# A two-layer streaming encoder step: first norm from token rows, parameter loads on two queues, another VectorE order in the FFN

## The chip, the cores and the metric

The kernel runs on 1 core of a Trainium2 chip. The metric is device time in microseconds (us) of one execution, smaller is better; TensorE is called PE here, VectorE DVE, ScalarE ACT, GpSimd POOL, SyncE SP.

## The reference

1,024 prompt frames and 32 frames of running streams, of width 1,024, go through two layers. Layer 0 mixes by a convolution module, layer 1 by attention in a sliding window; each mixer is followed by a gated FFN of inner width 2,816. Everything is in float32.

```python
def rms_norm(x, g):
    return x * lax.rsqrt(jnp.mean(x * x, axis=-1, keepdims=True) + RMS_EPS) * g
# layer 0
h = rms_norm(x, g_mix[0])
a, gate = jnp.split(h @ w_pw1 + b_pw1, 2, axis=-1)
g = concat([state or zeros, a * sigmoid(gate)])       # 30 frames of state
c = depthwise_conv31(g, w_dw) + b_dw
x = x + silu(layer_norm(c, ln_g, ln_b)) @ w_pw2 + b_pw2
x = x + (silu(h @ w_gate[0]) * (h @ w_up[0])) @ w_down[0]      # h = rms_norm(x, g_ffn[0])
# layer 1: 16 query heads, 4 key heads of 64, RMS norm of q and k per head
s = q @ k.T * SCALE - slope * distance, masked to own and two previous chunks of 64
p = exp(s - m) / (sum(exp(s - m)) + exp(sink - m))
x = x + (p @ v) @ w_o
x = x + FFN of layer 1
```

Also returned are the last 30 gated frames of both inputs and the last 128 keys and values.

## The kernel before, in words

The activations lie with channels on partitions: `x` holds 8 tiles (k = 0 to 7) of 128 channels by tokens. Tokens come in two halves, A (512) and B (512 and the 32 of the running streams, 544). A float32 product is made of three: every weight tile 128x1024 is loaded by SP into `raw` (two buffers), ACT's `hi()` (L795) copies it to `whi`, and POOL's `lo()` (L1797) takes the rest, `wlo`; activations likewise are split in `hAh`, `hAl`, `hBh`, `hBl`. A projection (`proj`) adds, for 8 tiles k, high·whi and low·whi (L327), and then 8 times high·wlo (L336). The FFN's way down does so with act·h and act·l (L522, L529).

PSUM's 8 banks are two rings of 4. A tile of half A takes one bank, one of half B two, so of B only two fit into a ring; a bank is taken when its user before it has freed it, in the order of the program.

**The start.** SP loads token rows `x_in` 0 to 8 into `stage`, ACT 17 small parameters into `R`. PE transposes x in groups of four 128x128 (`x_group`, L369), ACT (`x_in_place`, L878) and DVE (L1316) copy them to `x` and square them (`sqx`); PE sums the squares over channels with a matrix of ones (`square_mean`, L359), ACT makes Ln and Exp of the mean (`factor`), and `norm_parts` has DVE multiply (L1297), ACT copy the high half (`n_hi_part`), DVE subtract the low half (L1302). The second norm, `mix0B`, has its squares on ACT and their sums on POOL (`sum_squares`, L1807).

**SEQ1** is a list of 29 projections of `w_pw1`, gate and value in turn; half A's come first. Each pair is gated (`sigmoid`, L901, and `glu`), then the 31 taps of the convolution run beside: a tap is either a DVE operation in PSUM (L1389) or an ACT product (L920) added by POOL (L1828); `NP` says how many taps are products, `conv_a_steps` how many operations go beside each projection. At its end POOL's `csum` feeds the mean of the LayerNorm (L345 on PE). Then come `w_pw2` (p2) of half A, the FFN of half A with half B's convolution beside it, and so on: each half's FFN has the other half's mixer beside it.

**An FFN group** (`FFN 0A`, `0B`, `1A`, `1B`; G = 0 to 10) makes two pairs of gate and up projections and then, for the group before, eight tiles of the way down (D, d = 0 to 7), each added to x by DVE (`add_to_x`, L1468). Attention for the other half stands between, in steps of four units b: `read_scores` on DVE (L1496 to L1509), exps with their sums on ACT (`exps`, L1031), the division on DVE (`scale_probs`, L1533 and L1537), transposes, values, `out_low` on DVE. `act_low` (L1480) makes the low half of the gated activation. No planner sets the order; each engine's program lists it, and semaphores join the lists.

## Time and profile before

| what | us |
|---|---|
| time, median of 3 runs (range) | 2412.67 (2409.51 to 2414.92) |
| profiled execution, its own time | 2410.06 |
| profiled execution, span | 2408.2 |
| PE busy | 2284.0 (95%) |
| DVE busy | 1208.4 (50%) |
| POOL busy | 1120.4 (47%) |
| ACT busy | 979.0 (41%) |

The page has the span in slices, the chain of work that ended last, and groups of instructions with their releasers; "L327" is the source line. A duration stands in us, a mean in ns. A wait is put down to the event that came last. Matmuls are pipelined, so that the mean durations of their records overlap.

### The profile page before, as it was taken

The numbers are of one execution on the slowest core, as the hardware profiler recorded it, in microseconds if no ns is written. First come the engines' busy times: TensorE is split into PE (matmuls) and PEld (weight loads), VectorE is DVE, ScalarE is ACT, GpSimd is POOL, SyncE is SP. The second block draws the span as 40 slices with busy tenths as digits, with TensorE's granted clock in tenths as the row PEclk, the third lists the DMA queues.
The fourth block names the chain that finished last, engine by engine and source line by source line (L and its number), as shares of the span: only waits on it lengthen the run. The fifth ranks groups of instructions, "written<-read, shape, count | busy, mean of one in ns | idle before, by whom it ended". The sixth has DMA issues, their size and how long they took to land.

```text
span 2408.2 us, 34667 instructions
## 1 busy us (share of the span) xinstructions
PE 2284.0 (95%) x14027; PEld 2038.8 (85%) x14027; DVE 1208.4 (50%) x1924; ACT 979.0 (41%) x1511; POOL 1120.4 (47%) x588
## 2 busy tenths in 40 slices
PE   6897888999899999999999999999999999999999
PEld 5797666888789799899989889888888889999998
DVE  4687657883435335655563344556565342232233
ACT  4554644443423643433343356444444333222222
POOL 2799458996345533323233553333333343333332
PEclk8999899999999999999999999999999999999999
DMA  3111122233232322222222232222222322332222
GB/s 124 53 45 53 53 62 83 88 97 97 81 94 88 89 82 70 62 71 69 63 65 83 82 88 77 87 71 79 79 71 79 87 80 91 95 97 88 88 80 90
DMA packets 311436, 191.53 MB, mean 80 GB/s; under 512 B 40214, under 2 KB 285550, under 8 KB 311278
## 3 DMA queue, kind: packets, MB, share of 16 engines
q1 hardware_dynamic: 309168, 188.18, 26.3%
q8 instruction: 112, 1.84, 0.3%
q10 hardware_dynamic: 2110, 1.14, 0.2%
q14 instruction: 46, 0.38, 0.1%
HBM read 184.39 MB, written 5.10 MB: 79 GB/s over the span
## 4 chain that ended last, share of the span: by engine, by line
PE 81%; DVE 6%; POOL 6%; ACT 3%; issue 3%; DMA 0%; ACTq 0%; POOLq 0%; DVEq 0%
PE ps L327 37%; PE ps L336 19%; PE ps L522 12%; PE ps L529 6%; POOL accp L1828 4%; PE ps L492 2%; DVE x L1468 1%; PE ps L478 1%; PE ps L452 1%; PE ps L345 1%; PE ps L359 1%; DVE sco L1537 1%; DVE sq L1297 1%; POOL wlo L1797 1%; POOL rs L1807 1%
## 5 line engine op out<-in xcount | busy, mean ns | idle before, releaser
L1797 POOL TENSOR_TENSOR wlo<-raw,whi 128x1024 fp32r<-128x1024 f32 x342 | 825.4, 2414 | 1203.3 <-PE ps L336 838.9
L795 ACT ACTIVATE whi<-raw 128x1024 fp32r<-128x1024 f32 x342 | 361.4, 1057 | 715.0 <-PE ps L327 410.3
L327 PE MATMUL ps<-hBh,whi 128*128 128x272 f32 x2112 | 441.4, 290 | 16.2 <-ACT s L901 9.4
L327 PE MATMUL ps<-hAh,whi 128*128 128x512 f32 x1056 | 422.3, 400 | 34.9 <-DVE hAl L1302 15.5
L327 PE MATMUL ps<-hBl,whi 128*128 128x272 f32 x2112 | 439.9, 290 | 0.0
L327 PE MATMUL ps<-hAl,whi 128*128 128x512 f32 x1056 | 419.3, 397 | 0.0
L327 PEld LDWEIGHTS ps<-hBh,whi 128*128 128x128 f32 x2112 | 334.5, 190 | 19.8 <-ACT s L901 9.8
L1468 DVE TENSOR_TENSOR x<-ps,x 128x512 f32<-128x512 f32 (+1 forms) x368 | 252.2, 701 | 189.1 <-PE ps L529 131.3
L327 PEld LDWEIGHTS ps<-hBl,whi 128*128 128x128 f32 x2112 | 332.9, 189 | 0.0
L336 PE MATMUL ps<-hBh,wlo 128*128 128x272 f32 x2112 | 294.5, 292 | 0.0
L336 PEld LDWEIGHTS ps<-hBh,wlo 128*128 128x128 f32 x2112 | 273.5, 188 | 6.2 <-issue 1.9
L327 PEld LDWEIGHTS ps<-hAh,whi 128*128 128x128 f32 x1056 | 202.1, 191 | 89.4 <-issue 23.0
L336 PE MATMUL ps<-hAh,wlo 128*128 128x512 f32 x1056 | 273.5, 401 | 0.5 <-POOL wlo L1797 0.5
L1475 DVE TENSOR_TENSOR s<-ps,s 128x512 f32<-128x512 f32 (+1 forms) x88 | 62.3, 708 | 417.2 <-PE ps L336 415.2
L336 PEld LDWEIGHTS ps<-hAh,wlo 128*128 128x128 f32 x1056 | 196.4, 189 | 49.2 <-issue 4.3
L327 PEld LDWEIGHTS ps<-hAl,whi 128*128 128x128 f32 x1056 | 202.8, 192 | 40.9
L1828 POOL TENSOR_TENSOR accp<-accp,prod 128x512 f32<-128x512 f32 (+1 forms) x152 | 210.0, 1381 | 26.0 <-ACT prod L920 11.8
L1019 ACT ACTIVATE pth<-ps 128x512 fp32r<-128x512 f32 (+1 forms) x64 | 36.6, 571 | 194.1 <-PE ps L478 194.1
L1389 DVE SCALAR_TENSOR_TENSOR ps<-gxB,dwc,ps 128x574 f32<-128x574 f32 x152 | 113.9, 808 | 0.0
L1547 DVE TENSOR_TENSOR ptl<-ps,pth 128x512 fp32r<-128x512 f32 (+1 forms) x64 | 42.1, 658 | 122.5 <-ACT pth L1019 122.5
L1537 DVE TENSOR_SCALAR sco<-sco,small 128x256 f32<-128x256 f32 (+2 forms) x132 | 101.3, 809 | 2.3
L522 PE MATMUL ps<-act0h,whi 128*128 128x272 f32 (+1 forms) x288 | 79.0, 329 | 18.3 <-DVE x L1468 16.5
(233 smaller groups left out, 3277.4 us busy)
## 6 DMA issues: line engine op xcount, KB each, us to landing
raw<-in_w_gate_dram SPq DMA_DIRECT2D x88, 512.0 KB, 3.8
raw<-in_w_up_dram SPq DMA_DIRECT2D x88, 512.0 KB, 3.8
raw<-in_w_down_dram SPq DMA_DIRECT2D x88, 512.0 KB, 3.6
raw<-in_w_pw_dram SPq DMA_DIRECT2D x38, 512.0 KB, 4.0
raw<-in_w_qkv_dram SPq DMA_DIRECT2D x32, 256.0 KB, 3.7
raw<-in_w_o_dram SPq DMA_DIRECT2D x64, 128.0 KB, 2.9
stage<-in_x_prompt_dram SPq DMA_DIRECT2D x8, 512.0 KB, 7.7
raw<-in_w_qkv_dram SPq DMA_DIRECT2D x8, 512.0 KB, 3.7
```

Source lines behind the costliest of these rows:

```text
L327: ins = nc.tensor.matmul(o, whi[n % 2][:, P * k:P * (k + 1)], src[:, k, c0:c0 + w], start=(k == 0 and src is hi_[h]), stop=False)
L336: ins = nc.tensor.matmul(o, wlo[n % 2][:, P * k:P * (k + 1)], hi_[h][:, k, c0:c0 + w], start=False, stop=(k == KD - 1))
L492: ins = nc.tensor.matmul(ps[0:HD, 6, 0:256], v[:, slot, HD * g:HD * (g + 1)], p[:, 256 * z:256 * (z + 1)], start=(z == 0 and w == 0), stop ...
L522: ins = nc.tensor.matmul(o, whi[n % 2][:, wc], src[s + e][:, c0:c0 + w], start=(e == 0 and src is ach), stop=False)
L529: ins = nc.tensor.matmul(o, wlo[n % 2][:, wc], ach[s + e][:, c0:c0 + w], start=False, stop=(e == 1))
L795: nc.scalar.activation(whi[n % 2][:], raw[n % 2][:], ACT.Copy).then_inc(w_hi, 1)
L1389: link(nc.vector.scalar_tensor_tensor((X, Y)[q % 2], two(gx[h][:, c, t:t + w]), dwc[:, KD * t + c:KD * t + c + 1], (X, Y)[q % 2], ALU.mult ...
L1468: nc.vector.tensor_tensor(xd, pt(key), xd, ALU.add).then_inc(fr(key), 1)
L1475: nc.vector.tensor_tensor(s, pt(key), s, ALU.mult).then_inc(fr(key), 1)
L1537: ins = nc.vector.tensor_scalar(pr, pr, den[:, 2 * b + s:2 * b + s + 1], None, ALU.mult)
L1797: nc.gpsimd.tensor_tensor(wlo[n % 2][:], raw[n % 2][:], f(whi[n % 2][:]), ALU.subtract).then_inc(w_lo, 1)
L1828: nc.gpsimd.tensor_tensor(accp[p % 2][:, 0:w], accp[p % 2][:, 0:w], prod[r % 2][:, 0:w], ALU.add).then_inc(padd, 1)
```

## The change

In the first norm, ACT takes the square and its sum of each token row (`row_squares`, one value per token), Ln and Exp of it (`row_factor`), DVE makes of each 128 values a diagonal, and 32 float32 matmuls of a chunk of `stage` with a diagonal give the transposed and scaled x in PSUM (`xn`). ACT scales by the gain into the high half, DVE subtracts into the low half. For half B the diagonals are multiplied by ones on PE (`row_factors`) and copied to `rs`. The 17 parameter loads become 7 on ACT's queue and 8, with the sinks, on SP's; the later five x loads wait for `x_in[3]`; the distance, bias and mask work moves into later slots. Half A has one product less per channel and one chain operation more (10 for 11).

```python
-            want = 0 if s in (0, 1, 6) else 1 if s == 7 else 6 if s < 6 else 7
+            want = 0 if s < 2 else 1 if s in (5, 6) else 6 if s < 5 else 7
-NP = {"A": 11, "B": 10}
+NP = {"A": 10, "B": 10}
+            for k in range(KD):
+                b = take(("xn", k), "A", 1 - k % 2)
+                for t in range(4):
+                    pe.wait_ge(diag_ready, t + 1)
+                    ins = nc.tensor.matmul(ps[:, b, P * t:P * (t + 1)], stage[t][:, P * k:P * (k + 1)],
+                                           diag[:, t, :], start=True, stop=True)
+                ins.then_inc(pfull[b], 1)
...
+                nc.scalar.activation(junk[t % 2][0:w, :], stage[t][0:w, :], ACT.Square, accum_out=ssq[0:w, t:t + 1]
+                                     ).then_inc(row_sq, 1)
...
-                if s in (6, 7):
-                    if s == 6:
-                        factor("mix0B")
-                    for k in range(4 * (s - 6), 4 * (s - 5)):
+                if s in (5, 6):
+                    for k in range(4 * (s - 5), 4 * (s - 4)):
                         n_hi_part("mix0B", k)
...
             factor("ffn0A")
+            sigmoid(sig)
             for k in range(KD):
                 n_hi_part("ffn0A", k, ("p2", "A", KD - 1))
                 if k == 3:
-                    sigmoid(sig)
                     hi()
...
+                                if G == 1:
+                                    state_rows(b)
...
                         taps("B", CONV_B[G, 4][1])
-                        norm_b(G, 4)
...
+                        scale_probs(att, cur, 0)
                         exps(att, cur, 2)
+                        scale_probs(att, cur, 1)
                         exps(att, cur, 3)
                     if G:
                         hi()
+                    if (l, h) == (0, "A") and G:
+                        norm_b(G, 4)
...
+                    for d in range(KD):
+                        if G:
+                            add_to_x(("D", l, h, G - 1, d))
+                        if d == 1:
+                            read_scores(att, cur, 3)
+                        if d == 2:
+                            out_low(att, prev, 3)
+                        if d == 3:
+                            act_low(l, h, G, 1)
+                        if G and d % 2:
+                            denominators(att, cur, d // 2)
```

`scale_probs` is on ACT now, a Copy with a scale, after DVE's `denominators`, which is the reciprocal alone. The mean of `ffn0A` takes its bank before gate B2's projection, the mean of `lnB` ring 1; the state rows, four in a row after group 0, are spread over group 1's projections. POOL has seven `sum_squares` fewer.

PE at the start, before, from the parameters' transposes to the first two tiles of the first projection (L327 is `proj`, `sqx` the squares, `ones_d` the matrix of ones):

```order
L379 MATMUL ps<-ident,R 128x82 [waits pfree0,params_in]
L381 MATMUL ps<-ident,R 128x120 x2
L386 MATMUL ps<-ident,R 128x124 [waits pfree1]
L386 MATMUL ps<-ident,R 128x124
L359 MATMUL ps<-sqx,ones_d 128x512 [waits sq_ready,pfree2]
L359 MATMUL ps<-sqx,ones_d 128x512 [waits sq_dve]
L359 MATMUL ps<-sqx,ones_d 128x512 [waits sq_ready]
L359 MATMUL ps<-sqx,ones_d 128x512 [waits sq_dve]
L359 MATMUL ps<-sqx,ones_d 128x512 [waits sq_ready]
L359 MATMUL ps<-sqx,ones_d 128x512 [waits sq_dve]
```


And after, with one group of transposes behind the parameters and the diagonals (`diag`) as what streams through PE; L337 is `proj`:

```order
L403 MATMUL ps<-ident,R 128x40 [waits params_in]
L405 MATMUL ps<-ident,R 128x120 x2
L410 MATMUL ps<-ident,R 128x124 x2
L392 MATMUL ps<-ident,stage 128x128 [waits x_in3,pfree2]
L392 MATMUL ps<-ident,stage 128x128 x3
L392 MATMUL ps<-ident,stage 128x128 [waits pfree3]
L392 MATMUL ps<-ident,stage 128x128 x3
L418 MATMUL ps<-diag,stage 128x128 [waits diag_ready] x4
L418 MATMUL ps<-diag,stage 128x128 [waits diag_ready,pfree0]
L418 MATMUL ps<-diag,stage 128x128 [waits diag_ready] x7
```


The means of squares stood between the transposes and the projection; the diagonal matmuls stand there now, and none of them waits for `sqx`.

DVE at the end of an FFN group of half B with attention of half A (group 2 of FFN 0B), before: `out_low` (L1562) stands some rows higher, here stand the last score update, `act_low` (L1480), and then two sums into x (L1468), a reciprocal and two scalings for each pair:

```order
L1500 ISA small 128x1
L1509 TENSOR_SCALAR bias<-bias 128x256 [waits dv]
L1509 TENSOR_SCALAR bias<-bias 128x256
L1480 TENSOR_TENSOR act1l<-s,act1h 128x544 [waits act_hi]
L1468 TENSOR_TENSOR x<-ps,x 128x544 [waits pfull0]
L1468 TENSOR_TENSOR x<-ps,x 128x544 [waits pfull2]
L1533 RECIPROCAL small<-small 128x2 [waits e_ready]
L1537 TENSOR_SCALAR sco<-sco,small 128x128 [waits dv]
L1537 TENSOR_SCALAR sco<-sco,small 128x128
L1468 TENSOR_TENSOR x<-ps,x 128x544 [waits pfull0]
L1468 TENSOR_TENSOR x<-ps,x 128x544 [waits pfull2]
```


And after, behind two sums into x (not shown), where L1573 is `add_to_x`, L1637 the reciprocal, L1585 `act_low`, L1661 `out_low`, L1605 and L1614 `read_scores`:

```order
L1601 COPY sco<-nsink 128x2 [waits t_full]
L1605 ISA sco,small<-ps,bias,nsink 128x256 [waits s_full]
L1605 ISA small 128x1
L1605 ISA sco,small<-ps,bias,nsink 128x256
L1605 ISA small 128x1
L1614 TENSOR_SCALAR bias<-bias 128x256 [waits dv]
L1614 TENSOR_SCALAR bias<-bias 128x256
L1637 RECIPROCAL small<-small 128x2 [waits e_ready]
L1573 TENSOR_TENSOR x<-ps,x 128x544 [waits pfull2]
L1661 TENSOR_TENSOR hAl<-ps,hAh 64x2x128 [waits o_hi]
L1573 TENSOR_TENSOR x<-ps,x 128x544 [waits pfull0]
L1585 TENSOR_TENSOR act1l<-s,act1h 128x544 [waits act_hi]
```


Two sums stand ahead of the scores' read now, two more ahead of `act_low`, which stood ahead of all eight.

ACT at the end of the same kind of group, before: exps of four units (L1031, two each) and the two weight copies (L795):

```order
L1031 ACTIVATE sco,small<-sco,small 128x257 [waits s_read]
L1031 ACTIVATE sco,small<-sco,small 128x257
L795 ACTIVATE whi<-raw 128x1024 [waits whi_free,w_in0]
L1031 ACTIVATE sco,small<-sco,small 128x257 [waits s_read]
L1031 ACTIVATE sco,small<-sco,small 128x257
L1031 ACTIVATE sco,small<-sco,small 128x257 [waits s_read]
L1031 ACTIVATE sco,small<-sco,small 128x257
L795 ACTIVATE whi<-raw 128x1024 [waits whi_free,w_in1]
```


And after, where L840 is the weight copy, L1083 the exps and L1095 the scaling:

```order
L840 ACTIVATE whi<-raw 128x1024 [waits whi_free,w_in0]
L1095 ACTIVATE sco<-sco,small 128x128 [waits den_ready]
L1095 ACTIVATE sco<-sco,small 128x128
L1083 ACTIVATE sco,small<-sco,small 128x257 [waits s_read]
L1083 ACTIVATE sco,small<-sco,small 128x257
L1095 ACTIVATE sco<-sco,small 128x256 [waits den_ready]
L1095 ACTIVATE sco<-sco,small 128x256
L1083 ACTIVATE sco,small<-sco,small 128x257 [waits s_read]
L1083 ACTIVATE sco,small<-sco,small 128x257
L840 ACTIVATE whi<-raw 128x1024 [waits whi_free,w_in1]
L1095 ACTIVATE sco<-sco,small 128x256 [waits den_ready]
```


Scaling of units 0 and 1 stands between the exps of 1, 2 and 3 and thus ahead of the second weight copy; units 2 and 3 stand behind it.

## Rows read from the trace of the kernel before

**Rows 1.** Page, part 4: shares of the chain that ended last, by line.

```profile
PE ps L327 37%; PE ps L336 19%; PE ps L522 12%; PE ps L529 6%; POOL accp L1828 4%; PE ps L492 2%; DVE x L1468 1%; PE ps L478 1%; PE ps L452 1%; PE ps L345 1%; PE ps L359 1%; DVE sco L1537 1%; DVE sq L1297 1%; POOL wlo L1797 1%; POOL rs L1807 1%
```

**Rows 2.** Waits of PE, 0 to 350 us: total, times, longest (us).

```profile
PE ps L327 <- DVE hAl L1302: 15.5, 11, 7.1
PE ps L345 <- POOL csum L1850: 12.4, 1, 12.4
PE ps L327 <- ACT s L901: 9.4, 2, 9.2
PE ps L345 <- ACT s L901: 5.7, 1, 5.7
...
PE ps L379 <- DMA R<-in_state_conv_dram: 2.7, 1, 2.7
```

**Rows 3.** Timeline of the start: start, us, engine, what [idle before].

```profile
4.59 3.65 PE L369 MATMUL ps<-ident,stage 128*128 128x128 f32 x16 [4.59 <-DMA stage<-in_x_prompt_dram]
...
19.54 8.64 PE L359 MATMUL ps<-sqx,ones_d 128*128 128x512 f32 x16
...
28.27 1.28 ACT L819 ACT_TABLE_LOAD   x1 [8.02 <-PE ps L359]
...
33.34 0.77 PE L327 MATMUL ps<-hAh,whi 128*128 128x512 f32 x1 [5.16 <-DVE hAl L1302]
```

**Rows 4.** Timeline of PE alone: transposes of x, the mean after the convolution.

```profile
43.26 4.01 PE L369 MATMUL ps<-ident,stage 128*128 128x128 f32 x20
...
52.57 2.08 PE L369 MATMUL ps<-ident,stage 128*128 128x128 f32 x20
...
239.96 2.07 PE L345 MATMUL ps<-csum,ones_d 128*128 128x512 f32 x2 [12.40 <-POOL csum L1850]
```

**Rows 5.** Windows: each engine busy (instructions), PEclk, DMA share, GB/s.

```profile
19.50:22.80 3.30, 3.30 (x6) 1.40 (x5) 3.29 (x7) 0.75 (x1) 3.30 (x2) 0.51 0.10 40
22.90:28.20 5.30, 5.29 (x13) 2.06 (x11) 1.96 (x4) 0.00 (x0) 1.44 (x2) 1.00 0.68 198
33.30:47.30 14.00, 12.11 (x37) 8.78 (x38) 8.60 (x13) 6.00 (x10) 0.00 (x0) 0.52 0.00 1
367.00:403.00 36.00, 27.24 (x116) 20.72 (x115) 20.51 (x30) 15.76 (x23) 26.86 (x17) 0.95 0.27 80
```

**Rows 6.** Groups by line and shape: count, busy, mean ns, idle before.

```profile
L795 ACT ACTIVATE whi<-raw 128x1024 fp32r<-128x1024 f32 x342 | 361.4, 1057 | 715.0 <-PE ps L327 410.3 <-PE ps L522 301.4 <-DMA raw<-in_w_gate_dram 3.0
...
L1828 POOL TENSOR_TENSOR accp<-accp,prod 128x512 f32<-128x512 f32 x80 | 103.3, 1292 | 20.4 <-ACT prod L920 11.5 <-POOL accp L1828 0.4
L1389 DVE SCALAR_TENSOR_TENSOR ps<-gxA,dwc,ps 128x512 f32<-128x512 f32 x144 | 96.4, 747 | 0.0
...
L1031 ACT ACTIVATE sco<-sco,small 128x257 f32<-128x257 f32 x112 | 55.4, 498 | 0.1
```

**Rows 7.** Waits of PE, 350 to 800 us.

```profile
PE ps L327 <- ACT cvo L1232: 7.3, 4, 2.0
PE ps L327 <- ACT whi L795: 5.4, 1, 5.4
```

**Rows 8.** Chain of waits in order of time: start, us, piece.

```profile
654.89 6.77 PE ps L327 x16
...
734.99 4.03 PE ps L327 x32
```

**Rows 9.** Waits of PE, 800 to 1330 us.

```profile
PE ps L522 <- DVE x L1468: 23.2, 17, 2.2
```

**Rows 10.** Waits of PE, 1990 us to the end.

```profile
PE ps L522 <- DVE x L1468: 9.0, 10, 0.9
```

**Rows 11.** Timeline: two act_low of VectorE, one lo of GpSimd.

```profile
1063.25 0.71 DVE L1480 TENSOR_TENSOR act1l<-s,act1h 128x544 fp32r<-128x544 f32 x1
...
2112.79 1.58 DVE L1480 TENSOR_TENSOR act3l<-s,act3h 128x544 fp32r<-128x544 f32 x1 [0.72 <-ACT act3h L990]
...
2119.13 2.41 POOL L1797 TENSOR_TENSOR wlo<-raw,whi 128x1024 fp32r<-128x1024 f32 x1 [5.35 <-ACT whi L795]
```

More of the change, by code:

```diff
@@ L138, in build @@
             sqx = sb("sqx", [P, KD, 512], F32, c)
+        with ExitStack() as c:
+            junk = [sb(f"junk{s}", [P, D], F32, c) for s in range(2)]
+            diag = sb("diag", [P, 9, P], F32, c)
         with ExitStack() as c:
@@ L236, in pt @@
         def pt(key, rows=P):
-            b, _, h = place[key]
+            b, _, h, _ = place[key]
             if h == "A":
@@ L814, in factor @@
                 full(act, key)
-                if ev in ON_PE and i:
+                if ev in ON_PE:
                     old = EV[i - 1]
@@ L829, in n_hi_part @@
                     full(act, after)
-                act.wait_ge(xn_ready, KD * sum(e[:2] != "ln" for e in EV[:i]) + k + 1)
+                act.wait_ge(xn_ready, KD * sum(e[:2] != "ln" and e != "mix0A" for e in EV[:i]) + k + 1)
                 nc.scalar.activation(hi_[h][:, k, :], nrm[k % 2][:, dest(h)], ACT.Copy).then_inc(h_hi[h], 1)
@@ L1033, in exps, with scale_probs @@
                                          accum_out=den[:, 2 * b + s:2 * b + s + 1]).then_inc(e_ready, 1)
+            def scale_probs(h, beta, b):
+                if not 0 <= beta or b >= n_units(h, beta):
+                    return
+                u, _, _, _, _, nk, _ = unit(h, beta, b)
+                nk = nk if beta < 8 else WIN + TS
+                act.wait_ge(den_ready, u + 1)
+                for s in range(2):
+                    pr = sco[b][:, s, 1:1 + nk]
+                    ins = nc.scalar.activation(pr, pr, ACT.Copy, scale=den[:, 2 * b + s:2 * b + s + 1])
+                ins.then_inc(p_ready, 1)
             def q_high(h, i):
@@ new lines, in late_params @@
+            def late_params():
+                full(dve, ("par", 2))
+                b = place["par", 2][0]
+                nc.vector.tensor_copy(col[:, 40:NCOL], ps[:, b, 0:42]).then_inc(fr(("par", 2)), 1)
+                freed(dve, ("par", 2))
+                nc.vector.tensor_scalar(gqn, col[:, C_QN:C_QN + 1], -SCALE, None, ALU.mult).then_inc(col_ready, 1)
+                dve.wait_ge(sinks_in, 16)
+                for i in range(4):
+                    r = slice(TS * i, TS * (i + 1))
+                    ins = nc.vector.tensor_scalar(ssink[r, :], nsink[r, i:NH:4], -1.0, None, ALU.mult)
+                ins.then_inc(sink_ready, 1)
+                dve.wait_ge(sink_ready, 1)
+                nc.vector.tensor_scalar(nsink[:], nsink[:], -1.0, None, ALU.mult).then_inc(sink_ready, 1)
@@ L1681, in ffn @@
                         q_low(att, 7)
-                    out_low(att, prev, 3)
-                    read_scores(att, cur, 3)
-                    act_low(l, h, G, 1)
                     if (l, h, G) == (1, "A", NG - 1):
```

360 lines of the change are left out of this document (207 added, 153 removed).

## The prediction

> **What bounds the kernel now.** I read the chain that ended last first: over half of it is TensorE (PE) in the projections of L327 and L336, then the FFN's second product (L522, L529), and what is not PE is small and named: GpSimd's accp (POOL L1828) 4%, VectorE's sums into x (L1468) 1% [rows 1]. So the time is that of PE's work plus the gaps in it, and I price the change gap by gap. The waits of PE in the first 350 us show five large gaps, 45.7 us together: 15.5 behind the low halves of the first norm, 12.4 once behind GpSimd's csum at the end of the first convolution, 9.4 (9.2 of it in one wait, before the FFN's first projection) and 5.7 behind ScalarE's sigmoid, 2.7 behind the parameters' DMA [rows 2]. The rows of the start tell what the first gap is made of: transposes from 4.59 on, the means of the squares from 19.54, ScalarE's table at 28.27, the first projection at 33.34, and its first 16 matmuls spread out until 43.26, where the next transposes stand [rows 3, 4]. The clock there was 0.51 to 0.52 of full speed, that is the 1.2 GHz level, in the first 3.3 us of L359 and again from 33.3 to 47.3 [rows 5].
>
> **Part 1, the first norm (start to the convolution's mean).** Removed: transposes as the only source of the squares, L359's 8.64 us, and the chain VectorE, ScalarE, VectorE that paces the first projection, four pairs of channel tiles in 9.9 us (33.34 to 43.26). Added: a Square with sum for each of four token rows as they land. No row shows that; a copy of the same 128x1024 on ScalarE takes 1.06 [rows 6], twice that is my upper end; I take 1.24, near the copy. With x landing from 4.59 and a table load of 1.28 [rows 3], the squares end near 10.8 (10 to 15). Ln and Exp act on 4 columns, with the table 2.0: 12.8. Four diagonals and the parameter transposes lie beside or cost about 1: the diagonal matmuls start near 14. They leave 64 records (32 matmuls, two records each). The nearest rows are the 20 transposes of the same tile: 0.104 each at 52.57, 0.20 each at 43.26 [rows 4], so 6.7 if all run at the upper level and 12.8 if none does. L359 began at 0.51 for 3.3 us and ran on at 1.00 [rows 5]; treated so, 16 records take 3.3 and 48 take 5.0, 8.3. New weights in each could cost more, so I take 10.5 (6.7 to 20): 24.5. The 16 matmuls of the first projection then stand behind one another, 3.8 with the last low half: they end near 28.4, not 43.26: **-15**.
>
> The Trainium skill (TensorE: Matmul & The Clock Gate, Part 4: PE-mode transpose) says that transposes don't count as PE work for the clock gate. The trace agrees so far as L359 ran at 0.51 right behind 32 transposes; by that rule the diagonal matmuls begin low, and without it the step would take 6.7, 3.8 less than in my sum.
>
> From there to the mean at 239.96 [rows 4]: the 5.7 wait (GpSimd's sums of squares for the second norm, which go) is gone, and the x transposes at 43.26 take 2.08, not 4.01 [rows 2, 4]. But ScalarE and VectorE have more squares and diagonals at the same steps, so I give 1.5 back: **-6**. Then the 12.4 wait. GpSimd loses 8 products of 1.29 [rows 6] and seven sums, of about the same length by shape: 10.3 + 9.3 = 19.6. With a start 15 earlier it could end 35 earlier; PE, with 21 off, is what would stop it, and VectorE gains 8 operations of 0.67 (96.4/144) [rows 6], 5.4 us, and in the last step 17 in place of 11. So the wait shrinks, it doesn't go: 12.4 to 7.5: **-5**. In all **-26** (-10, if GpSimd or the second norm holds PE as before, to -35).
>
> **Part 2, parameters on two queues.** The 2.7 wait lies in the 15 already: it is off the path once diagonals are later than landing. What moves, iota, biases and masks, goes to ScalarE and GpSimd in the second stage's norm slots, where both wait for PE; without that cover it is 8 ScalarE operations and 13 small ones of GpSimd, some 5 us. On SP's queue the small loads stand ahead of x4 to x8, which now also wait for x3; PE first needs x4 one projection later than before. **0** (0 to +3).
>
> **Part 3, the FFN's first norm and the state rows.** The sigmoid now stands before the norm's parts and the bank is taken earlier, so the 9.2 wait ends when the mean and its Ln and Exp do, 2.7 behind: **-6.5** (-3 to -8). The state rows are spread over the next group's projections: in 367 to 403 PE was busy 27.24 of 36 [rows 5], 7.3 of the rest in four waits for ScalarE's cvo [rows 7]. Spread, each copy has a projection for cover: **-9** (-6 to -11). In group 8, ScalarE's weight copies stood behind the norm's parts: 5.4 [rows 7], and the 16 matmuls behind took 6.77 where 32 of 272 columns take 4.03 [rows 8], by columns 3.8 for these, so 3.0 more at the low clock. With the copies first: **-8** (-5 to -8.4).
>
> **Part 4, FFN order and scaling.** In FFN 0B PE waits 23.2 in 17 waits for L1468 [rows 9]; VectorE was late because read_scores, act_low and scaling stood between sums into x. Now two sums come first, then read_scores, sums, out_low, act_low. Scaling leaves VectorE; on ScalarE a 128x257 pass takes 0.498 [rows 6], so 132 passes of a little less cost some 60 us of ScalarE's idle time: 0 while the second weight copy isn't held up. What is late next is act_low: at 1063.25 it took 0.71, at 2112.79 1.58, with GpSimd's L1797 beside it (2.41 long, as at 2119.13) [rows 11]. By the new order two sums 1.5 apart, the read of the scores, a reciprocal, two more sums and out_low come ahead of it: it starts 7.1 behind the first sum in 0B by my estimate, GpSimd's low weights at 6.9: held to 9.3, ended at 9.9, which costs PE 1.6 and with the read before it 1.85 a group; ten groups, 18.5 against 23.2: **-5** (-20 if VectorE starts first, 0 if more is held). In FFN 1B there are ten waits, 9.0 in all [rows 10]; the pieces before act_low are fewer there, it starts 0.06 before GpSimd: **-9** (+7 if behind, 1.6 for each group).
>
> **Sum**: -26 - 6.5 - 9 - 8 - 5 - 9 = -63.5 from the profiled execution's own 2410.06 (span 2408.2): 2346.6. The median of before, 2412.67, is 2.6 above that execution; I add half of this: **2348**.
>
> **Rivals.** (a) *GpSimd first in both FFNs.* Every act_low in the third place stands behind L1797: FFN 0B gives 0, FFN 1B costs 7, and with a start worth 18 only: 2410 - 18 - 6.5 - 9 - 8 + 7 = 2375. For it: the 1.58 row; against: 0.71 is as often seen, and in 1B the order by 0.06 us is mine, from a schedule that shifts. The Trainium skill (SBUF — State Buffer, Who interferes with whom) says that a VectorE operation with two SBUF inputs shares a read port with GpSimd, that one of them waits for the other's end, and that sums with one input in PSUM don't. The two act_low rows agree. Rows 11 alone give the 1.6.
> (b) *VectorE first in both, and the start at its better end*: -30 - 7 - 9 - 8 - 20 - 9 = -83, 2327. For it: VectorE's share is 50% and it loses all of L1537. Against: the first part's copies.
> (c) *Slower: ScalarE's queue.* It runs in order; scaling unit 1 waits for VectorE's reciprocal, behind act_low, and ahead of it stand the last exps and the second weight copy. If that copy comes over a projection late (4.03 for 32 of its 48 matmuls, so 6 us), PE waits as at group 8, 5.4 + 3.0 = 8.4 [rows 7, 8], in each of 20 groups with attention: +168, and with the gains of parts 1 and 3, 2410 - 49.5 + 168 = 2529; it decides from the point where the reciprocal is 6 us late. Against: act_low held by GpSimd is 2.4 late, and the second copy waits for PE to free its buffer anyway.
> (d) *The start's gain doesn't arrive*: the second norm and GpSimd hold PE in the first stage until the mean stands where it stood, part 3 gives its least, 3 + 6 + 5, and act_low costs its 7: 2410 - 14 + 7 = 2403, at the edge of no change. For it: GpSimd is the releaser of the 12.4; against: it loses 19.6 of work before that.
>
> **How the numbers follow.** Forecast 0.53, its own range 2335 to 2365; (a) 0.22; (b) 0.16; (c) 0.06; (d) 0.03. The range 2320 to 2385 takes in (a), (b), the forecast and the ends of the diagonal matmuls' cost, and leaves out (c), (d) and the tails. About 0.2% (5 us) is what a measurement here tells from no change: faster 0.53 + 0.22 + 0.16 = 0.91, same 0.03, slower 0.06.
>
> **What would show it.** Right: the first L327 near 25 and the mean of the convolution near 214, not 239.96; waits for cvo and for the weight copy at group 8 gone; L1468's waits in 0B about 18, in 1B near 0, with VectorE's act_low there 0.71 long. A clock at half level under the diagonal matmuls makes part 1 6 to 8 us worse. Act_low at 1.6 to 2.4 in 1B is (a). Wrong: PE waiting for whi in the attention groups (c), or the csum wait still over 12 (d).

## The result, and the profile after

The changed kernel takes 2324.2 us, median of four runs (2323.93 to 2325.04), against 2411.59 (2409.51 to 2414.92) for the kernel before on the same chip: a ratio of 0.9637, 95% interval 0.9620 to 0.9654, 87 us less. 2348 was forecast, with a range of 2320 to 2385. The time lies in the range, outside the forecast's own range (2335 to 2365), and 3 us from rival (b), 2327.

The profiled execution spans 2322.2 us, 86.0 less than before. By the page's totals PE is busy 2263.4 us instead of 2284.0, so 65.4 of the 86.0 us is idle time (124.2 us before, 58.8 after). How much of the other 20.6 is less work and how much the clock the totals don't tell; the mean granted clock was 0.983 before and 0.989 after. The page's chain, shares by line:

```profile
PE ps L337 41%; PE ps L346 21%; PE ps L553 14%; PE ps L560 7%; PE ps L523 2%; POOL accp L1920 2%; PE ps L483 1%; PE ps L509 1%; PE ps L355 1%; PE ps L484 1%; PE ps L485 1%; POOL wlo L1889 1%; PE ps L372 1%; DVE x L1573 1%; DVE sq L1382 1%
```

Against [rows 1] the projections' shares (L337 and L346 are L327 and L336 of before) grew by 4 and 2 points, and the scaling on VectorE has left the chain.

Where the 86 us came from, by the start of an instruction that both traces have:

```
                                             before    after    shift   in the stage   forecast
mean after the first convolution             239.96   214.12   -25.8      -25.8         -26
first way down (D) of FFN 0A                 402.58   358.41   -44.2      -18.3         -6.5 - 9
last way down of FFN 0A                      712.57   661.69   -50.9       -6.7         -8
first way down of FFN 0B                     916.11   866.53   -49.6       +1.3          0
first way down of FFN 1A                    1538.17  1466.73   -71.4      -21.9         -5
first way down of FFN 1B                    2034.54  1961.71   -72.8       -1.4          0
end of the span                             2408.2   2322.2    -86.0      -13.2         -9
```

Two stages carry the miss: FFN 0B, 17 us more than forecast, and FFN 1B, 4 more. The +1.3 is a stretch of PE at a granted clock of 0.60, so mostly at the 1.2 GHz level (768.4 to 772.0), behind a wait of 1.9; the runs below with the squares early, with the same program there, don't have it, and why it comes is not shown.

The start. These are rows of the timeline of PE (start, duration, what, idle time before it), for what [rows 3, 4] show of before:

```profile
16.42 9.27 PE L418 MATMUL ps<-diag,stage 128*128 128x128 f32 x64 [1.61 <-DVE diag L1415]
25.45 0.48 PE L337 MATMUL ps<-hAh,whi 128*128 128x512 f32 x1
...
35.04 2.35 PE L392 MATMUL ps<-ident,stage 128*128 128x128 f32 x20
...
214.12 2.08 PE L355 MATMUL ps<-csum,ones_d 128*128 128x512 f32 x2 [9.01 <-POOL csum L1942]
```

The diagonal matmuls start at 16.4, 2.4 later than forecast, take 9.27 where 10.5 was taken, and the first projection starts at 25.45 (24.5 forecast). What they waited for stands in VectorE's rows:

```profile
13.19 0.20 DVE L1407 COPY col<-ps 128x40 f32<-128x40 f32 x1 [2.56 <-PE ps L405]
...
15.46 1.50 DVE L1415 TENSOR_SCALAR diag<-ident,small 128x128 f32<-128x128 f32 x4
```

The factor was there at 12.34. PE's transposes of the parameters waited for their DMA until 12.54; VectorE stood idle 2.56 us for them, then copied the parameters (13.19) and the two groups of x that PE transposes behind them, and only then made the diagonals.

The 16 matmuls of the first projection stand one behind the other until 29.3; before it was 43.26. The windows of PE (length, then busy time of PE, PEld, DVE, ACT, POOL, then the clock) show that the first 2.6 us of L418 ran at the 1.2 GHz level, as L359 had begun [rows 5]:

```profile
16.40:19.00 2.60, 2.58 (x12) 2.58 (x13) 0.56 (x3) 0.46 (x1) 0.00 (x0) 0.50 1.01 413
19.00:25.70 6.70, 6.70 (x55) 6.70 (x55) 4.46 (x7) 5.08 (x8) 2.37 (x1) 0.90 0.48 147
```

The waits of PE, first from 0 to 300 us, then from 300 to 750 and from 750 to 1300 (total, times, longest):

```profile
PE ps L355 <- POOL csum L1942: 9.0, 1, 9.0
PE ps L337 <- DVE hAl L1387: 8.3, 7, 7.1
PE ps L337 <- ACT s L951: 4.8, 1, 4.8
...
PE ps L403 <- DMA R<-in_state_conv_dram: 2.6, 1, 2.6
...
PE ps L346 <- POOL wlo L1889: 2.9, 1, 2.9
PE ps L337 <- DVE hAl L1387: 2.6, 2, 1.3
...
PE ps L553 <- DVE x L1573: 3.9, 3, 1.3
```

Of [rows 2] the low halves of the first norm are gone (8.3 is the next norm's, 7.1 of it one wait; of the 15.5 of before 8.2 were that norm's already), the wait for csum fell from 12.4 to 9.0, and the one before the FFN from 9.2 to 2.6 in two. The 5.7 for a sigmoid is not gone: PE waits 4.8 for one at 65.12, its only wait above a microsecond between the first projection and the one for csum. Two others that the kernel before had in this stretch are gone:

```profile
PE ps L327 <- ACT whi L795: 2.9, 1, 2.9
PE ps L327 <- DVE gxA L1350: 0.9, 1, 0.9
```

Of [rows 7] both are gone, but a wait for GpSimd's low weights, 2.9, is new. The sums into x held PE 17 times for 23.2 us in FFN 0B [rows 9] and now 3 times for 3.9; in FFN 1B ten times for 9.0 [rows 10], and now not once (1900 us to the end).

**A wait costs more than its length.** In FFN 1B the waits were 0.9 each, but each group became 1.2 shorter. Rows of PE's timeline, of before and then of after, from the first matmul of a way down to the projection behind it:

```profile
2111.07 0.42 PE L522 MATMUL ps<-act0h,whi 128*128 128x272 f32 x2
...
2115.15 0.49 PE L522 MATMUL ps<-act0h,whi 128*128 128x272 f32 x2 [0.89 <-DVE x L1468]
...
2124.29 0.42 PE L327 MATMUL ps<-hBh,whi 128*128 128x272 f32 x2
```

```profile
2035.74 0.41 PE L553 MATMUL ps<-act0h,whi 128*128 128x272 f32 x2
...
2047.75 0.41 PE L337 MATMUL ps<-hBh,whi 128*128 128x272 f32 x2
```

2124.29 - 2111.07 = 13.22 and 2047.75 - 2035.74 = 12.01: 1.21 for a wait of 0.89, so 0.3 more, which the profile shows as no idle time. In ten groups that is 3.2 of the 4 us that FFN 1B gave beyond its forecast.

**In FFN 0B a race decides.** Two groups of FFN 0B, timeline of VectorE, GpSimd and PE:

```profile
1002.04 0.72 DVE L1573 TENSOR_TENSOR x<-ps,x 128x544 f32<-128x544 f32 x1 [1.40 <-PE ps L560]
...
1006.27 0.42 DVE L1661 TENSOR_TENSOR hAl<-ps,hAh 64x256 fp32r<-64x256 f32 x1
...
1007.23 2.40 POOL L1889 TENSOR_TENSOR wlo<-raw,whi 128x1024 fp32r<-128x1024 f32 x1 [4.87 <-ACT whi L840]
1007.36 2.85 DVE L1585 TENSOR_TENSOR act1l<-s,act1h 128x544 fp32r<-128x544 f32 x1
...
1011.06 0.49 PE L553 MATMUL ps<-act2h,whi 128*128 128x272 f32 x2 [1.31 <-DVE x L1573]
...
1094.36 0.72 DVE L1573 TENSOR_TENSOR x<-ps,x 128x544 f32<-128x544 f32 x1 [1.40 <-PE ps L560]
...
1098.48 0.40 DVE L1661 TENSOR_TENSOR hAl<-ps,hAh 64x256 fp32r<-64x256 f32 x1
...
1099.50 0.71 DVE L1585 TENSOR_TENSOR act1l<-s,act1h 128x544 fp32r<-128x544 f32 x1
1099.55 2.94 POOL L1889 TENSOR_TENSOR wlo<-raw,whi 128x1024 fp32r<-128x1024 f32 x1 [4.87 <-ACT whi L840]
```

The rows at 1002.04 and 1094.36 are the first sums of the two groups. In the first group GpSimd starts 0.13 ahead, VectorE's act_low lasts 2.85, and PE waits 1.31. In the second group VectorE starts 0.05 ahead, act_low lasts 0.71, GpSimd is the one that is longer (2.94 for 2.40), and PE doesn't wait. Of the eight groups with attention and a way down, three are like the first (a way down of 13.8 us) and five like the second (12.2 to 12.3; before, 15.3 and once 16.0). The prediction had GpSimd first in all.

Which groups lose is no chance: GpSimd starts 5.19 behind the first sum in both, and VectorE comes 0.18 later in the first because of `out_low` (L1661). It starts 0.73 behind the start of the sum ahead of it (1005.54), not 0.62 (1097.86), and the next sum 0.45 behind it, not 0.38. The three groups are those whose `out_low` finishes an odd key head and so writes to partitions 64 to 127 (`r = slice(HD * (g % 2), ...)` in the kernel); four of the five have an even one, and the first has none. The same groups have the longer steps in the runs below. Why the one for an odd head starts later is open.

### The profile page after: what moved, and what is told of

Same layout as the page of the kernel before. It is cut to its first block, busy times and chain, and to the rows that moved or that the text cites. A ratio compares the mean times of both kernels' runs of the same rounds, so it can differ in the third digit from the quotient of the medians.

```text
span 2322.2 us, 34761 instructions
## 1 busy us (share of the span) xinstructions
PE 2263.4 (97%) x14082; PEld 2034.6 (88%) x14082; DVE 1096.5 (47%) x1802; ACT 1024.8 (44%) x1639; POOL 1114.9 (48%) x573
## 3 DMA queue, kind: packets, MB, share of 16 engines
q8 instruction: 113, 1.85, 0.3%
## 4 chain that ended last, share of the span: by engine, by line
PE 91%; POOL 3%; DVE 2%; ACT 2%; issue 1%; DMA 0%; ACTq 0%; DVEq 0%; POOLq 0%
PE ps L337 41%; PE ps L346 21%; PE ps L553 14%; PE ps L560 7%; PE ps L523 2%; POOL accp L1920 2%; PE ps L483 1%; PE ps L509 1%; PE ps L355 1%; PE ps L484 1%; PE ps L485 1%; POOL wlo L1889 1%; PE ps L372 1%; DVE x L1573 1%; DVE sq L1382 1%
## 5 line engine op out<-in xcount | busy, mean ns | idle before, releaser
L1889 POOL TENSOR_TENSOR wlo<-raw,whi 128x1024 fp32r<-128x1024 f32 x342 | 839.7, 2455 | 1131.6 <-PE ps L346 802.9
L840 ACT ACTIVATE whi<-raw 128x1024 fp32r<-128x1024 f32 x342 | 361.6, 1057 | 638.7 <-PE ps L337 379.7
L337 PE MATMUL ps<-hBh,whi 128*128 128x272 f32 x2112 | 440.2, 289 | 8.2 <-DVE x L1573 3.3
L337 PE MATMUL ps<-hBl,whi 128*128 128x272 f32 x2112 | 439.4, 289 | 0.0
L337 PE MATMUL ps<-hAh,whi 128*128 128x512 f32 x1056 | 417.9, 396 | 18.5 <-DVE hAl L1387 10.9
L337 PE MATMUL ps<-hAl,whi 128*128 128x512 f32 x1056 | 415.4, 393 | 0.0
L1573 DVE TENSOR_TENSOR x<-ps,x 128x512 f32<-128x512 f32 (+1 forms) x368 | 258.3, 705 | 243.9 <-PE ps L560 181.4
L337 PEld LDWEIGHTS ps<-hBh,whi 128*128 128x128 f32 x2112 | 332.9, 189 | 11.4 <-issue 5.0
L337 PEld LDWEIGHTS ps<-hBl,whi 128*128 128x128 f32 x2112 | 331.6, 189 | 0.0
L346 PE MATMUL ps<-hBh,wlo 128*128 128x272 f32 x2112 | 293.7, 291 | 0.0
L346 PEld LDWEIGHTS ps<-hBh,wlo 128*128 128x128 f32 x2112 | 273.0, 188 | 6.3 <-issue 1.9
L346 PE MATMUL ps<-hAh,wlo 128*128 128x512 f32 x1056 | 275.0, 403 | 2.9 <-POOL wlo L1889 2.9
L337 PEld LDWEIGHTS ps<-hAh,whi 128*128 128x128 f32 x1056 | 200.3, 190 | 67.9 <-DVE hAl L1387 11.1
L346 PEld LDWEIGHTS ps<-hAh,wlo 128*128 128x128 f32 x1056 | 196.7, 190 | 51.7 <-issue 4.3
L337 PEld LDWEIGHTS ps<-hAl,whi 128*128 128x128 f32 x1056 | 200.8, 190 | 39.9
L1920 POOL TENSOR_TENSOR accp<-accp,prod 128x512 f32<-128x512 f32 (+1 forms) x144 | 200.2, 1390 | 25.3 <-ACT prod L970 12.5
L1489 DVE SCALAR_TENSOR_TENSOR ps<-gxA,dwc,ps 128x512 f32<-128x512 f32 x152 | 101.8, 748 | 0.0
```

The lines of the kernel that those rows point to most:

```text
L337: ins = nc.tensor.matmul(o, whi[n % 2][:, P * k:P * (k + 1)], src[:, k, c0:c0 + w], start=(k == 0 and src is hi_[h]), stop=False)
L346: ins = nc.tensor.matmul(o, wlo[n % 2][:, P * k:P * (k + 1)], hi_[h][:, k, c0:c0 + w], start=False, stop=(k == KD - 1))
L840: nc.scalar.activation(whi[n % 2][:], raw[n % 2][:], ACT.Copy).then_inc(w_hi, 1)
L1489: link(nc.vector.scalar_tensor_tensor((X, Y)[q % 2], two(gx[h][:, c, t:t + w]), dwc[:, KD * t + c:KD * t + c + 1], (X, Y)[q % 2], ALU.mult ...
L1573: nc.vector.tensor_tensor(xd, pt(key), xd, ALU.add).then_inc(fr(key), 1)
L1889: nc.gpsimd.tensor_tensor(wlo[n % 2][:], raw[n % 2][:], f(whi[n % 2][:]), ALU.subtract).then_inc(w_lo, 1)
```

## The experiments

All start from the changed kernel (2324.2) and were timed in three rounds beside the kernel before, whose median was 2409.35 to 2411.18 there and 2411.59 above. A difference of 2 or 3 us between two runs is therefore read from the traces too.

### The reciprocal ahead of act_low

```diff
+                        if G and d % 2:
+                            denominators(att, cur, d // 2)
                         if d == 3:
                             act_low(l, h, G, 1)
-                        if G and d % 2:
-                            denominators(att, cur, d // 2)
```

> The changed kernel with one swap: at the fourth sum into x, VectorE's reciprocal (0.15 us) stands before act_low instead of behind it. In the changed kernel act_low of FFN 0B starts 0.05 us before GpSimd's low weights in five groups with attention (0.71 long) and 0.13 behind in three (2.85 long); the way down takes 12.24 us in the five and 13.80 in the three. Theory, who starts first decides: all eight are now behind, act_low about 2.8 long, the way down 13.8 in all eight, +5 x 1.56 = 8, so about 2332 us. FFN 1A's act_low is held too, without a wait of TensorE; FFN 1B has no reciprocal there and stays. Rival, the three long ones have another cause (the data's landing, the banks): five short, three long as before, 2324 within 2.

Measured 2323.71 us (ratio 0.9639, 0.9625 to 0.9653): unchanged, the rival's number. Timeline of a group of this kernel:

```profile
918.61 3.00 POOL L1889 TENSOR_TENSOR wlo<-raw,whi 128x1024 fp32r<-128x1024 f32 x1 [4.87 <-ACT whi L840]
918.63 0.70 DVE L1585 TENSOR_TENSOR act1l<-s,act1h 128x544 fp32r<-128x544 f32 x1
```

The reciprocal is 0.15 long, but the next instruction started only 0.07 behind it. GpSimd's recorded start is now 0.02 ahead, and VectorE is served first all the same. The same three groups stayed long (0.20 ahead, 2.78). In FFN 1A of this run a lead of 0.06 wasn't enough either (1513.87 and 1513.93; act_low 0.66 long). So the recorded starts don't tell who is first within some hundredths of a microsecond; in these rows the point lies between 0.06 and 0.13 of GpSimd's lead. The run doesn't speak for the rival's reason, the landing of data or the banks, since act_low was hardly moved; what sets the three apart is `out_low`, as above.

### act_low earlier

```diff
                         if d == 2:
+                            act_low(l, h, G, 1)
                             out_low(att, prev, 3)
-                        if d == 3:
-                            act_low(l, h, G, 1)
```

> The changed kernel with act_low at the third sum into x, ahead of out_low, about 1.1 us earlier. Theory, start decides: VectorE is first in every group with attention, act_low 0.7 long in all of FFN 0B, no wait of TensorE for the sums there, 3 x 1.56 = 4.7 less: about 2319.5 us. Rival, out_low or the fourth sum, now 0.7 later, is missed by TensorE instead (by the values of the next unit or by the two slots of the ring): 2324 or more.

Measured 2319.96 us (0.9623, 0.9609 to 0.9637). Act_low is 0.71 long in every group of FFN 0B, and PE's waits from 750 to 1300 us have no row for the sums any more.

4.2 us of the 4.7 expected: the three groups with an odd key head take 12.47 now, not 12.24. With about a microsecond to spare instead of hundredths, the race is gone.

### act_low later

```diff
-                        if d == 3:
+                        if d == 4:
                             act_low(l, h, G, 1)
```

> The changed kernel with act_low one sum later, behind the fifth. GpSimd's low weights are then always first, by about 1.5 us of their 2.4, so act_low is held for the rest and takes about 1.6 in all eight groups with attention of FFN 0B and the like in FFN 1B. Theory, what costs is where the hold falls: act_low ends about 8.25 behind the first sum, the sixth sum ends at 9.0, and the eighth tile takes that bank at 9.0: no wait or under 0.1, the three waits of the changed kernel go too: 2324.2 - 4.7 = 2319.5 us. Rival, being held is what costs: a wait of about 1 in each of eighteen groups, 2340 us.

Measured 2321.35 us (0.9630, 0.9616 to 0.9645). A group of it, VectorE and GpSimd:

```profile
1007.47 2.42 POOL L1889 TENSOR_TENSOR wlo<-raw,whi 128x1024 fp32r<-128x1024 f32 x1 [4.87 <-ACT whi L840]
...
1009.16 1.30 DVE L1585 TENSOR_TENSOR act1l<-s,act1h 128x544 fp32r<-128x544 f32 x1
```

Act_low starts 1.69 behind GpSimd (1.58 to 1.79 in the others) and is held for the rest of GpSimd's 2.42, in every group of FFN 0B, and PE's matmuls have no recorded wait for a sum. So a hold alone doesn't cost the 1.3; a hold that spans the next two sums does: 2.85 ahead of the fifth did, 1.30 ahead of the sixth doesn't. But it isn't free. In FFN 1B, where no group lost the race before, act_low is now held for 1.54, and each way down takes 12.24 to 12.29 instead of 12.01. One of them, PE and its weight loads, up to the projection behind it:

```profile
2030.90 0.41 PE L553 MATMUL ps<-act0h,whi 128*128 128x272 f32 x2
...
2041.53 0.30 PEld L553 LDWEIGHTS ps<-act0h,whi 128*128 128x128 f32 x2 [0.19 <-DVE x L1573]
...
2043.14 0.41 PE L337 MATMUL ps<-hBh,whi 128*128 128x272 f32 x2
```

The weight load of the eighth tile waits 0.19 for the held sum. In ten groups that is some 2.5 us, and FFN 1B's stage is 3.0 longer; this is the step that the expectation left out, and why the run ends 1.9 above its 2319.5.

### A delay ahead of act_low

```diff
+        pad = sb("pad", [P, 8])
...
                         if d == 3:
+                            if att and G:
+                                for z in range(4):
+                                    nc.vector.tensor_copy(pad[:, 2 * z:2 * z + 2], nsink[:, 2 * z:2 * z + 2])
                             act_low(l, h, G, 1)
```

> The changed kernel with four copies of 128x2 (about 0.07 us apart, into a scratch tile) on VectorE ahead of act_low at the fourth sum, in groups with attention: act_low starts about 0.3 later. With the reciprocal ahead it came only 0.07 later, GpSimd's recorded start was 0.02 ahead and act_low still took 0.70; at 0.13 ahead it takes 2.85. Theory, who starts first decides: now GpSimd is over 0.2 ahead in all eight groups of FFN 0B, act_low 2.6 to 2.8 in all eight, TensorE waits 1.2 to 1.3 in each, and 0.3 of refilling: +5 x 1.56 + 3 x 0 = 8, 2332 us. Rival, the three long ones have another cause: three long, five short, 2324 to 2326.

Measured 2341.61 us (0.9720, 0.9705 to 0.9734): 17.4 slower, not 8, and not in the way expected. Timeline of a group, VectorE, GpSimd and PE:

```profile
921.73 2.58 DVE L1796 COPY pad<-nsink 128x2 f32<-128x2 f32 x4
921.79 2.43 POOL L1893 TENSOR_TENSOR wlo<-raw,whi 128x1024 fp32r<-128x1024 f32 x1 [4.91 <-ACT whi L841]
924.23 0.71 DVE L1586 TENSOR_TENSOR act1l<-s,act1h 128x544 fp32r<-128x544 f32 x1
...
925.79 0.49 PE L554 MATMUL ps<-act2h,whi 128*128 128x272 f32 x2 [1.41 <-DVE x L1574]
```

It was a copy that was held: the four copies of two columns, meant to take 0.3 us, lasted 2.58, to the end of GpSimd's instruction; one of them took 2.38, the others 0.16 each, and act_low behind them was short. The waits came in all the eight groups (1.3 to 1.6), and also in the two groups behind them, so that 12.4 of the 17.4 were lost from FFN 0B to FFN 1A. Of the rest 2.3 lie in FFN 1A, where the copies stand too, and 2.5 ahead of the first copy, where kernels with the same program differ by about as much (2.2 between the changed kernel and the one with act_low earlier). The Trainium skill (SBUF — State Buffer, Who interferes with whom) says that a copy too can take both port pairs and then waits for GpSimd to end; the 2.38 agrees. As a probe of act_low alone the run failed; that a VectorE instruction behind GpSimd's start costs PE 1.4 us at this place it does show.

### The old order, and the old place of the scaling

The first undoes the order of VectorE and leaves the scaling on ScalarE:

```diff
+                    out_low(att, prev, 3)
+                    read_scores(att, cur, 3)
+                    act_low(l, h, G, 1)
                     for d in range(KD):
                         if G:
                             add_to_x(("D", l, h, G - 1, d))
-                        if d == 1:
-                            read_scores(att, cur, 3)
-                        if d == 2:
-                            out_low(att, prev, 3)
-                        if d == 3:
-                            act_low(l, h, G, 1)
```

> The changed kernel with VectorE's order of before at the end of a group (out_low, the read of the fourth unit's scores and act_low ahead of all eight sums into x), with the scaling left on ScalarE. Theory, the order is worth most: TensorE waits again at the third tile in each of the eight groups with attention of FFN 0B, 1.5 and 0.3 for refilling, 14.6, and in FFN 1B's ten, 0.9 and 0.3, 12.3; the wait of 1.3 at the seventh tile stays gone, and the three held act_low go: 2324 + 14.6 + 12.3 - 4.7 = 2346 us. Rival, it was the scaling that made VectorE late: FFN 0B has no more than 3 us of waits, and only FFN 1B's 12.3 come back: 2332 to 2337.

Measured 2347.8 us (0.9740, 0.9724 to 0.9757), for 2346 expected. Its waits of PE for the sums, 750 to 1300 us and then from 1900 on:

```profile
PE ps L553 <- DVE x L1573: 13.8, 10, 2.2
...
PE ps L553 <- DVE x L1573: 9.0, 10, 0.9
```

FFN 0B has one wait for each group again, at the third tile, and FFN 1B its ten of 0.9. The second wait of the kernel before, 1.3 at the seventh tile, stays gone: there the two scalings ahead of the sum took 2.69 beside GpSimd's low weights (1068.86 in the trace of before), and they don't stand there now. By stages the run lost 8.4 us in FFN 0B and 11.5 in FFN 1B, a little less than expected, and 3.3 in FFN 0A, which the expectation didn't have; so the 2346 was met in part by luck.

The second puts the scaling back behind the reciprocal on VectorE and takes ScalarE's away:

```diff
             def denominators(h, beta, b):
                 ...
-                nc.vector.reciprocal(den[:, 2 * b:2 * b + 2], den[:, 2 * b:2 * b + 2]).then_inc(den_ready, 1)
+                link(nc.vector.reciprocal(den[:, 2 * b:2 * b + 2], den[:, 2 * b:2 * b + 2]))
+                linked()
...
+                for s in range(2):
+                    pr = sco[b][:, s, 1:1 + nk]
+                    ins = nc.vector.tensor_scalar(pr, pr, den[:, 2 * b + s:2 * b + s + 1], None, ALU.mult)
+                ins.then_inc(p_ready, 1)
```

> The changed kernel with the scaling of probabilities back on VectorE behind each reciprocal, the new order of sums kept. Theory, scaling is held behind GpSimd's low weights (2.69 us for two in the kernel before) and makes the sums late: in each of the eight groups with attention TensorE waits 1.3 to 3 and 0.3 for refilling, 13 to 26 in all: 2337 to 2350 us; FFN 1B unchanged. Rival, VectorE has room for it once two sums stand ahead: 2324 within 3.

Measured 2337.67 us (0.9695, 0.9681 to 0.9710). PE waits for the sums from 750 to 1300 us, two waits (0.5 and 1.4) for each of eight groups:

```profile
PE ps L553 <- DVE x L1568: 15.7, 16, 1.5
```

The time is as expected, the mechanism only in part. GpSimd and VectorE in one of the eight groups:

```profile
1109.18 2.40 POOL L1891 TENSOR_TENSOR wlo<-raw,whi 128x1024 fp32r<-128x1024 f32 x1 [4.87 <-ACT whi L840]
...
1109.60 2.57 DVE L1580 TENSOR_TENSOR act1l<-s,act1h 128x544 fp32r<-128x544 f32 x1
```

The scaling ahead of the sums is not held (0.48 for two, at 1107.61). It makes act_low late, which now loses the race in all eight groups (2.3 to 2.9 long) and brings the wait of 1.4; the 0.5 is a sum late behind the scaling. So each half of the edit alone leaves a wait in every group: the order is worth 23.6 us (20 of them in FFN 0B and 1B), the scaling 13.5 in FFN 0B. The scaling's worth hangs on where act_low stands; with act_low earlier it was not tried.

### The squares of the convolution's second norm early

```diff
                         taps("B", CONV_B[G, 4][1])
+                        if G < 8:
+                            norm_b(G, 4)
...
-                    if (l, h) == (0, "A") and G:
+                    if (l, h) == (0, "A") and G >= 8:
                         norm_b(G, 4)
```

> The changed kernel with one half of an edit undone: the fifth part of the convolution's second norm stands behind both weight copies on ScalarE only from group 8 on; in groups 1 to 7 (in group 6 these are squares of channels 2 and 3) it stands ahead of the exps and copies as before. Theory, the squares behind the copies made GpSimd's sums late, so that the low weights behind them came 2.9 us late for TensorE, and the clock fell after it: the shift against the kernel before goes back by 4.5 there. With the squares early again -4.5: 2319.7 us, with no wait for the weight copy at group 8. Rival, the squares wait for VectorE's sums into x, which now stand first, and hold the copies: TensorE waits for a weight copy in group 6, 5 us or more, 2324 to 2330.

Measured 2318.66 us (0.9623, 0.9609 to 0.9637), 5.5 less. ScalarE's squares of channels 2 and 3 in the changed kernel, with GpSimd's sums and low weights and PE's matmuls behind them, and then the same squares in this one:

```profile
536.82 1.19 ACT L854 ACTIVATE sq<-gxB 128x544 f32<-128x544 f32 x2
537.54 2.87 POOL L1899 TENSOR_TENSOR rs<-rs,sq 128x544 f32<-128x544 f32 x2 [9.76 <-ACT sq L854]
...
540.36 4.67 POOL L1889 TENSOR_TENSOR wlo<-raw,whi 128x1024 fp32r<-128x1024 f32 x2
...
542.76 3.60 PE L346 MATMUL ps<-hAh,wlo 128*128 128x512 f32 x8 [2.92 <-POOL wlo L1889]
```

```profile
526.11 1.19 ACT L854 ACTIVATE sq<-gxB 128x544 f32<-128x544 f32 x2
```

Behind the two weight copies the squares came 10 us later, GpSimd stood waiting for them (9.76) with two low weights queued behind, and PE found the first of them 2.9 late. The eight matmuls behind that wait take 3.60, where eight of the same kind take 2.1 elsewhere; the granted clock was 0.57 from 542.7 to 546.5, mostly the 1.2 GHz level. By the trace the wait and the slow stretch are worth 4.7 us at this place. With the squares early that wait is gone, and so is any for a weight copy in group 8. The move was meant for group 8 alone.

### The state rows in one piece

```diff
-                                if G == 1:
-                                    state_rows(b)
...
+                    if (l, h, G) == (0, "A", 0):
+                        for j in range(4):
+                            state_rows(j)
...
```

That is PE's part; ScalarE's copies go back likewise (not shown).

> The changed kernel with the state rows back in one piece after the first group, and their copies on ScalarE where they were. Theory: the four waits for cvo, 7.3, come back, with their low clock: +9, 2333 us. Rival: most of the 18 us that the stretch from the FFN's first norm to the first way down gave is the sigmoid's move, and the state rows are worth 2 or 3: 2327.

Measured 2335.05 us (0.9690, 0.9674 to 0.9706): 10.9 more, and the four waits are back. PE from 300 to 750 us:

```profile
PE ps L337 <- ACT cvo L1302: 7.6, 4, 2.3
```

### One product more for each channel

```diff
-NP = {"A": 10, "B": 10}
+NP = {"A": 11, "B": 10}
```

> The changed kernel with 11 products for each channel of half A's convolution, as before, in place of 10 (8 more sums on GpSimd, 8 chain operations fewer on VectorE, in the last step 9 in place of 17). Theory of the prediction, GpSimd's whole work ends last: the csum wait grows from 9.0 by 8 x 1.3 = 10, 2334 us. Rival, GpSimd has room in the steps before (it is busy 88% from 100 to 200 us) and only the last step's one sum more counts, 1.4: 2325.6.

Measured 2330.84 us (0.9672, 0.9658 to 0.9686), 6.6 more: between the two. Waits of PE, 0 to 300 us:

```profile
PE ps L355 <- POOL csum L1942: 10.8, 1, 10.8
...
PE ps L337 <- ACT s L951: 5.7, 1, 5.7
...
PE ps L337 <- DVE gxB L1456: 0.7, 1, 0.7
PE ps L337 <- ACT whi L840: 0.5, 1, 0.5
```

The mean comes at 219.9 instead of 214.1. Of the 5.8 us 1.8 are in the csum wait, the rest in smaller waits before it, for ScalarE's weight copies and sigmoids and for the gating, and in the clock that falls after them. At the end VectorE stood idle 5.79 us for GpSimd's last sum, in the changed kernel 0.95. ScalarE's products for GpSimd stand in the same queue as the copies; that a slow sum holds these through the products was not tried by itself.

### The two edits together, and the convolution's operations earlier

The first has act_low early and the squares early:

> Two edits together: act_low early (measured alone 2319.96 us) and the squares early (2318.66). They lie in different FFNs. Theory, they add: 2324.2 - 4.2 - 5.5 = 2314.5 us. Rival, the one moves what the other frees: 2318 or more.

Measured 2313.82 us (0.9597, 0.9583 to 0.9612): they add. The second has in addition

```diff
-            want = 0 if s < 2 else 1 if s in (5, 6) else 6 if s < 5 else 7
+            want = 0 if s < 2 else 1 if s in (5, 6) else 6 if s < 5 else 8
```

> As the two edits together, and from the eighth projection on 8 operations of half A's convolution beside each projection in place of 7, so that fewer are left for the last step (17 before). Theory, the 9.0 us csum wait is the last step's 15 chain operations on VectorE and 6 sums on GpSimd: with a few operations left it falls to about 3 or 4, 2309 us. Rival, VectorE (busy 42 to 45 of 50 us beside these projections) and GpSimd fall behind earlier and hold ScalarE's products, and through its queue the weight copies and sigmoids: TensorE waits there instead, 2314 or more.

Measured 2304.9 us (0.9561, 0.9545 to 0.9577), 8.9 less than without and the best of all, 19.3 below the changed kernel. The last step has no operation left. The mean after the convolution, and PE's waits for the sigmoid from 0 to 300 us:

```profile
205.94 1.12 PE L355 MATMUL ps<-csum,ones_d 128*128 128x512 f32 x2
```

```profile
PE ps L337 <- ACT s L951: 6.7, 3, 4.8
```

The wait for csum is gone altogether, for 1.9 us of two new waits for sigmoids. The rival named a real price, but a small one.

## Why the prediction was right, and where not

**The start** (-26, measured -25.8) was right as a whole, but its three pieces were off and cancel, which is luck: -15, -6 and -5 were forecast; -14.0 (43.26 to 29.28), -8.5 and -3.4 came. In the first piece the diagonals came 2.4 later than forecast, with squares and factor as worked out, and the diagonal matmuls were 1.2 shorter, with the low clock at their beginning. In the second the 5.7 wait was counted as gone and is a wait of 4.8; in its place two waits went that the sum didn't have, 2.9 for a weight copy and 0.9 for the gating, and the transposes took 2.35 for 4.01. In the third the csum wait was forecast at 7.5 and is 9.0. That the last step bounds it, not GpSimd's work as a whole, is shown by the run with 8 operations; that GpSimd's work counts too, by the run with 11 products: 6.6 us for 8 sums of 1.3. The prediction also read the 15.5 of [rows 2] as the first norm's alone; 8.2 of it belong to the LayerNorm, which the change leaves as it was. No term hung on it, the -15 being worked out from [rows 3, 4]. No run undoes the new first norm by itself, so the -14.0 is read from the two traces alone.

**Parameters** were put at 0, "off the path once diagonals are later than landing". That step failed by some 2.4 us inside the start: the diagonals were later than the landing because of it, since VectorE's copies of the parameters and of x, queued ahead of the diagonals, waited for PE, which waited 2.64 for the parameters. No run takes the wait away by itself.

**FFN's first norm and the state rows** gave 18.3 for 15.5. The state rows alone are worth 10.9 (9 forecast), which leaves 7.4 for the norm (6.5).

**Group 8** was forecast at -8 with the copies first. That gain came, and more: with the squares early the stage gives -11.5 by that run's trace, of which 0.8 is one more wait that went (for ScalarE's rs) and the rest of the 3.5 isn't accounted for. But the same line moves the squares of group 6, and these put a wait of 2.9 on GpSimd's low weights, 4.8 on the stage and 5.5 on the time: -6.7 in all. The step that failed counted one of the two places where the moved call does something.

**FFN 0B** is where the forecast failed in size: -5 forecast, -21.9 measured. The failing step is the sentence that act_low "starts 7.1 behind the first sum in 0B by my estimate, GpSimd's low weights at 6.9". They start 5.14 (or 5.32) and 5.19 behind it, by the rows of the two groups above. The price of losing was right: 13.80 - 12.00 (a group of FFN 1B, which has no scores to read) = 1.80 for 1.85. But three groups pay it, where ten were counted, and five pay 0.24. An estimate with an error of 2 us could not decide an order of 0.05; the term had two values, -5 and -20, and the forecast took one of them. The ten ways down of FFN 0B are 22.4 us shorter: 19.3 of it are recorded waits (23.2 - 3.9), and 3.1 stand beside them, which the forecast, counting waits alone, didn't have.

**FFN 1B**: -9 forecast, -13.2 measured; the waits went as forecast, VectorE being 0.05 first in the groups (0.06 forecast), and the 0.3 for each makes most of the difference. That the order came out is in part luck: the same kind of estimate was off by 2 us in FFN 0B.

**Rival (a)** describes the three groups, **rival (b)** came nearest in its time and describes the other five and FFN 1B, **(c)** didn't occur: no wait for a weight copy in the attention groups, though ScalarE took over the scaling of 132 pieces. **(d)** didn't occur.

## What to carry to other kernels

When two engines can hold each other, look for the distance between their starts before giving a price: if an estimate can't tell the order, the forecast has two values, and an edit that moves the sensitive instruction by a microsecond, to either side, is worth more than the estimate. Earlier was the better side here: later, the held instruction cost 0.24 us in each group of FFN 1B. A wait of PE is worth its length and, here, up to 0.3 us more. When a call is moved for one of its uses, list what it does at the others.

## What the runs showed of the hardware

- GpSimd's lead in recorded starts had to be more than 0.02 to 0.06 us to hold act_low (reciprocal ahead: 0.70 and 0.66 long); 0.13 held it (2.85). The recorded start isn't the whole of it: with the scaling on VectorE one act_low 0.25 behind GpSimd (1737.79) is 0.67 long. The one that comes second waits for the end of the other's instruction: 2.85 for 0.71 on VectorE, 2.94 for 2.40 on GpSimd.
- A VectorE copy of 128x2 with its source in SBUF is held by GpSimd like an operation with two SBUF inputs: one of four took 2.38, the others 0.16 each.
- VectorE's `out_low` of 64x256 starts 0.73 behind the start of the sum ahead of it when its result goes to partitions 64 to 127, 0.62 when it goes to 0 to 63.
- A stall of PE of 0.9 us lengthens a way down by 1.2 (FFN 1B, 13.22 and 12.01).
